# Dissolving the pooling stage into the linear attention stage, and holding the slab pairs by stage

## The reference, cut to what matters

```
p, gla_q, gla_k, gla_v, gla_g, r_f, r_b, q, k, v = split_in(rmsnorm(x) modulated @ w_in)
pooled:  for each of 4 groups of 64 columns, window w in (2, 4, 8, 16):
         m = mean over the window around each token - the token itself
         pooled = (m @ w_pool[group]) * s_pool
linear attention (gla): gates la = log_sigmoid(r @ w_gate + b_gate) / 16, in two directions;
         o = causal decayed attention forwards + strict one backwards; rmsnorm(o, g_gla) * silu(gla_g)
attention: q, k = rmsnorm per head of 64, times g_q, g_k; axial_rope on the latent tokens; softmax attention
```

## Time and profile before

| what | value |
|---|---|
| median of three runs | 4188.84 us |
| the profiled execution's own time | 4184.54 us |
| its span, first to last instruction | 4182.7 us |
| TensorE busy, share of the span | 86% |
| VectorE, ScalarE, GpSimd busy | 54%, 30%, 28% |
| mean granted TensorE clock | 0.917 |
| pooling stage, layer 0 and layer 1, from VectorE's first instruction to that of the next stage | 43.95 us, 44.82 us |
| linear attention, the same | 177.94 us, 144.72 us |

### The profile page before, as it was taken

The page is one execution under the profiler, slowest core; times in us unless marked ns, Lnnn a source line. Parts: engine busy times, 40 slices in busy tenths (PEclk is TensorE's granted clock), DMA queues, the critical chain, the costliest instruction groups (busy, mean ns, idle before and its releaser), DMA issues. The chain is left out here.

```text
span 4182.7 us, 56917 instructions
## 1 busy us (share of the span) xinstructions
PE 3584.2 (86%) x22004; PEld 2999.0 (72%) x22004; DVE 2271.7 (54%) x3290; ACT 1249.8 (30%) x1868; POOL 1160.9 (28%) x564
## 2 busy tenths in 40 slices
PE   6955697899998965798997899888988986887998
PEld 4745576788887745677885788767777775775886
DVE  4658562655655347545445588723666766336334
ACT  4113322221222113323223345432333432323222
POOL 4205002232222203014442333143231230423442
PEclk7977898999999977899998999999999998998998
DMA  4420001223222420013331121121111110212221
GB/s 162 166 79 1 1 1 61 76 96 111 107 85 88 166 79 1 1 41 116 116 115 54 66 70 65 46 91 61 46 42 36 46 37 11 96 65 71 96 95 60
DMA packets 85333, 295.30 MB, mean 71 GB/s; under 512 B 13507, under 2 KB 14083, under 8 KB 84741
## 3 DMA queue, kind: packets, MB, share of 16 engines
q1 hardware_dynamic: 84836, 290.74, 19.7%
q10 hardware_dynamic: 288, 1.60, 0.1%
HBM read 290.21 MB, written 2.10 MB: 70 GB/s over the span
## 5 line engine op out<-in xcount | busy, mean ns | idle before, releaser
L222 POOL TENSOR_TENSOR slab_lo<-slab,slab_hi 128x1024 fp32r<-128x1024 f32 x330 | 823.8, 2502 | 2273.1 <-ACT slab_hi L205 2273.1
L205 ACT ACTIVATE slab_hi<-slab 128x1024 fp32r<-128x1024 f32 x330 | 346.2, 1056 | 792.7 <-PE banks L121 473.7
L119 PE MATMUL banks<-hT_hi,slab_hi 128*128 128x512 f32 (+1 forms) x896 | 354.7, 396 | 44.7 <-POOL slab_lo L222 34.3
L120 PE MATMUL banks<-hT_lo,slab_hi 128*128 128x512 f32 (+1 forms) x896 | 349.5, 390 | 0.0
L121 PE MATMUL banks<-hT_hi,slab_lo 128*128 128x512 f32 (+1 forms) x896 | 349.0, 389 | 0.0
L119 PE MATMUL banks<-mlp_hid_hi,slab_hi 128*128 128x512 f32 (+1 forms) x768 | 282.0, 367 | 10.1 <-DVE mlp_hid_lo L1794 10.1
L1794 DVE TENSOR_TENSOR mlp_hid_lo<-mlp_sq,mlp_hid_hi 128x512 fp32r<-128x512 f32 (+1 forms) x96 | 216.6, 2257 | 120.9 <-ACT mlp_hid_hi L1752 120.5
L120 PE MATMUL banks<-mlp_hid_lo,slab_hi 128*128 128x512 f32 (+1 forms) x768 | 279.6, 364 | 0.0
L121 PE MATMUL banks<-mlp_hid_hi,slab_lo 128*128 128x512 f32 (+1 forms) x768 | 279.4, 364 | 0.0
L119 PE MATMUL banks<-slab_hi,hT_hi 128*128 128x256 f32 (+1 forms) x728 | 246.4, 338 | 2.5 <-ACT rT L872 2.5
L119 PEld LDWEIGHTS banks<-hT_hi,slab_hi 128*128 128x128 f32 x896 | 172.4, 192 | 82.1 <-POOL slab_lo L222 35.7
(11 more groups left out here) (552 smaller groups left out, 8251.7 us busy)
## 6 DMA issues: line engine op xcount, KB each, us to landing
slab<-in_s_mlp_dram SPq DMA_DIRECT2D x192, 512.0 KB, 3.6
proj_vec_slab<-in_s_vec_proj_dram SPq DMA_DIRECT2D x64, 512.0 KB, 3.6
mlp_vec_slab<-in_s_vec_mlp_dram SPq DMA_DIRECT2D x64, 512.0 KB, 3.5
slab<-in_s_ssm_dram SPq DMA_DIRECT2D x48, 512.0 KB, 3.5
slab<-in_s_gdn_dram SPq DMA_DIRECT2D x48, 512.0 KB, 3.5
slab<-in_s_in_dram SPq DMA_DIRECT2D x32, 512.0 KB, 4.6
slab<-in_s_out_dram SPq DMA_DIRECT2D x24, 512.0 KB, 3.7
slab<-in_s_merge_ssm_dram SPq DMA_DIRECT2D x24, 512.0 KB, 3.5
```

Source lines behind the costliest of these rows:

```text
L119: nc.tensor.matmul(out, lhs.hi, rhs.hi, start=start, stop=False)
L120: nc.tensor.matmul(out, lhs.hi, rhs.lo, start=False, stop=False)
L205: self.nc.scalar.activation(hi, self.raw[s][:], ACT.Copy).then_inc(self.rounded, 1)
L222: self.nc.gpsimd.tensor_tensor(pair.lo[:], self.raw[u % slots][:], pair.hi[:].bitcast(F32), ALU.subtract).then_inc(self.split, 1)
```

## The change

The stage `pooling` is removed, and each of its instructions stands in `gla`, spread over its parts:

- SyncE issues the band, gains, rope table and w_pool behind the four loads of the gate weights.
- ScalarE squares q and k in two instructions (tiles 0 to 3 into r3, 4 and 5 into r2) before everything else; the root stands behind the six Abs; the means of the first two groups are moved behind Ln, those of the other two between the exponents of level 1 and level 2. The scaling by s_pool is now ScalarE's, behind the exponents of levels 5 and 8.
- VectorE sums the squares, takes the reciprocal, multiplies by root and gains, and rotates tile 2, all before the gates. It clears F and rotates tile 3 directly behind the gates, before the own products; tiles 4 and 5 are rotated behind the decayed keys, before the masks of the states.
- TensorE makes the first two groups' means behind the gate logits, the others' behind the own products, and mixes behind the products of levels 3 and 6. Banks 6 and 7 are kept for this, so the level products go round six banks.
- The stage's semaphores are 26 before and 37 after; pooling had 12, attention has 11, the end of modulation 1 and the projection 21.
- Ring holds no pairs of its own. Each stage that streams slabs (modulation start, projection, out and post product, mlp, merge, and now also the two scans of the second block) takes as many as it uses, four or three, from its own memory. The added tensors of `gla` lie in the memory that this leaves free.

The diff, cut to its core (the removed function is printed above):

```
-    SLOTS, PAIRS = 4, 3
+    SLOTS = 4
...
-        self.pairs = [sbuf_pair(ctx.enter_context, nc, f"slab{s}", [P, D]) for s in range(self.PAIRS)]
...
-    def fourth_pair(self, stage):
-
-        self.pairs[3:] = [sbuf_pair(stage.held.enter_context, self.nc, f"{stage.name}_slab3", [P, D])]
+    def hold_pairs(self, stage):
+
+        self.pairs = [sbuf_pair(stage.held.enter_context, self.nc, f"{stage.name}_slab{n}", [P, D]) for n in range(self.shape(self.at)[3])]
...
+        m_ = [sb(f"m{n}", [P, TOK]) for n in range(2)]
...
+        qk_sq = [(0, 4, r3[:, 0:4 * nqk * HD]), (4, 6, r2[:, 0:2 * nqk * HD])]
+        pool_loads, wp_loads, qk_loads, wp_cleared, means, moved, mixed, pooled = (sem(n) for n in
+            ("pool_loads", "wp_loads", "qk_loads", "wp_cleared", "means", "moved", "mixed", "pooled"))
+        qk_squared, qk_summed, qk_root = (sem(n) for n in ("qk_squared", "qk_summed", "qk_root"))
...
+                sp.dma_start(rope[:], a["rope"].rearrange("p (s t f) -> p s t f", s=2, t=LAT_TILES)).then_inc(qk_loads, 16)
+                sp.wait_ge(wp_cleared, 2)
+                for g in range(4):
+                    o_ = 64 * (g % 2)
+                    sp.dma_start(wp[o_:o_ + 64, g // 2, o_:o_ + 64], a["w_pool"][l, g]).then_inc(wp_loads, 16)
...
+                def pool_means(pair):
+
+                    if pair:
+                        pe.wait_ge(moved, 3)
+                    else:
+                        pe.wait_ge(pool_loads, 16 + 1)
+                    for n, (t0, t1) in enumerate(((CTX_TILES, C), (0, CTX_TILES))):
+                        for gg_ in range(2):
+                            g = 2 * pair + gg_
+                            for t in range(t0, t1):
+                                same = 0 if t == t0 else 2 if t == t1 - 1 else 1
+                                terms = [(t, same)] + [(t - 1, 3)] * (t > t0) + [(t + 1, 4)] * (t < t1 - 1)
+                                for e, (src, kind) in enumerate(terms):
+                                    last = nc.tensor.matmul(c.ps[64 * gg_:64 * gg_ + 64, 6 + n, (t - t0) * P:(t - t0 + 1) * P],
+                                                            c.tok[:, src, C_POOL + 64 * g:C_POOL + 64 * g + 64],
+                                                            bands[:, kind, g, :], start=e == 0, stop=e == len(terms) - 1)
+                        last.then_inc(means, 1)
+
+                def pool_mix(pair):
+                    pe.wait_ge(wp_loads, 16 * 4 + 1)
+                    pe.wait_ge(moved, 5)
+                    if pair:
+                        pe.wait_ge(pooled, 3)
+                    for n, s in enumerate((slice(CTX, TOK), slice(0, CTX))):
+                        nc.tensor.matmul(c.ps[:, 6 + n, 0:s.stop - s.start], wp[:, pair, :], m_[pair][:, s], start=True, stop=True).then_inc(mixed, 1)
...
+                pool_means(0)
...
+                pool_means(1)
...
                         pe.wait_ge(own_read, nb + 1)
                     for n in range(nb // 2):
                         done = (lev - 1) * (nb // 2) + n
-                        if done >= 8:
-                            pe.wait_ge(a_read, done - 6)
+                        if done >= 6:
+                            pe.wait_ge(a_read, done - 4)
                         for e in range(4):
                             ch = first + 2 * n + e // 2
-                            last = nc.tensor.matmul(c.ps[:, done % 8, e * P:(e + 1) * P].rearrange("p (h f) -> p h f", h=2),
+                            last = nc.tensor.matmul(c.ps[:, done % 6, e * P:(e + 1) * P].rearrange("p (h f) -> p h f", h=2),
                                                     F[:, lev % 2, e % 2, ch * P:(ch + 1) * P], Q[:, lev % 2, :, e % 2, ch, :], start=True, stop=True)
                         last.then_inc(a_full, 1)
+                    if lev in (3, 6):
+                        pool_mix(lev // 3 - 1)
                 pe.wait_ge(a_read, LEVELS * nb + 1)
...
+                def pool_moved(pair):
+                    for n, s in enumerate((slice(CTX, TOK), slice(0, CTX))):
+                        act.wait_ge(means, 2 * pair + n + 2)
+                        nc.scalar.activation(m_[pair][:, s], c.ps[:, 6 + n, 0:s.stop - s.start], ACT.Copy).then_inc(moved, 1)
+
+                def pool_out(pair):
+                    for n, s in enumerate((slice(CTX, TOK), slice(0, CTX))):
+                        act.wait_ge(mixed, 2 * pair + n + 2)
+                        nc.scalar.activation(c.pooled[:, pair, s], c.ps[:, 6 + n, 0:s.stop - s.start], ACT.Copy,
+                                             scale=c.small(l, "s_pool")[:, pair:pair + 1]).then_inc(pooled, 1)
+
+                for t0, t1, sq_ in qk_sq:
+                    nc.scalar.activation(sq_.rearrange("p (t n) -> p t n", t=t1 - t0), x[:, t0:t1], ACT.Square).then_inc(qk_squared, 1)
                 for t in range(C):
                     act.wait_ge(logits, t + 2)
                     nc.scalar.activation(t0_[:, t, :], c.ps[:, t, :], ACT.Abs).then_inc(exps, 1)
+                act.wait_ge(qk_summed, 3)
+                nc.scalar.activation(qk_stat[:, 1, :], qk_stat[:, 0, :], ACT.Sqrt, bias=c.eps, scale=1.0 / HD).then_inc(qk_root, 1)
...
+                pool_moved(0)
...
+                    if lev == 1:
+                        pool_moved(1)
+                    if lev in (5, 8):
+                        pool_out(lev // 3 - 1)
...
+                nc.vector.memset(wp[:], 0.0).then_inc(wp_cleared, 1)
...
+                def rotate(t):
+                    xv = x[:, t].rearrange("p (h r s f) -> p h r s f", h=nqk, r=2, s=2)
+                    x1, x2 = xv[:, :, :, 0, :], xv[:, :, :, 1, :]
+                    cs, sn = (rope[:, j, t - CTX_TILES, :].rearrange("p (r f) -> p r f", r=2).unsqueeze(1).to_broadcast([P, nqk, 2, 16])
+                              for j in range(2))
+                    nc.vector.tensor_tensor(rot[:, 0], x1, sn, ALU.mult)
+                    link(nc.vector.tensor_tensor(rot[:, 1], x2, sn, ALU.mult))
+                    nc.vector.tensor_tensor(x1, x1, cs, ALU.mult)
+                    link(nc.vector.tensor_tensor(x2, x2, cs, ALU.mult))
+                    nc.vector.tensor_tensor(x1, x1, rot[:, 1], ALU.subtract)
+                    link(nc.vector.tensor_tensor(x2, x2, rot[:, 0], ALU.add))
+
+                for n, (t0, t1, sq_) in enumerate(qk_sq):
+                    dve.wait_ge(qk_squared, n + 2)
+                    nc.vector.tensor_reduce(qk_stat[:, 0, t0 * nqk:t1 * nqk], sq_.rearrange("p (n e) -> p n e", e=HD), AX, ALU.add).then_inc(qk_summed, 1)
+                dve.wait_ge(qk_root, 2)
+                link(nc.vector.reciprocal(qk_stat[:, 2, :], qk_stat[:, 1, :]))
+                for t in range(C):
+                    last = nc.vector.tensor_tensor(heads(t), heads(t), qk_stat[:, 2, t * nqk:(t + 1) * nqk].unsqueeze(2).to_broadcast([P, nqk, HD]), ALU.mult)
+                link(last)
+                dve.wait_ge(qk_loads, 49)
+                for t in range(C):
+                    last = nc.vector.tensor_tensor(heads(t), heads(t), g_qk[:], ALU.mult)
+                link(last)
+                rotate(2)
                 dve.wait_ge(exps, C + 3)
                 for t in range(C):
 
                     link(nc.vector.scalar_tensor_tensor(out=la[:, t, :], in0=c.ps[:, t, :], scalar=0.0, in1=t0_[:, t, :],
                                                         op0=ALU.min, op1=ALU.subtract))
                     nc.vector.tensor_scalar(la[:, t, :], la[:, t, :], 1.0 / 16, None, ALU.mult).then_inc(la_ready, 1)
+                dve.wait_ge(la_ready, C + 1)
+                nc.vector.memset(F, 0.0).then_inc(cleared, 1)
+                rotate(3)
 
...
-                nc.vector.memset(F, 0.0).then_inc(cleared, 1)
...
                         last = nc.vector.tensor_tensor(kd[:, 2 * d:2 * d + 2, s], kd[:, 2 * d:2 * d + 2, s], c.gqk[:, 2:4, s], ALU.mult)
                     last.then_inc(kd_ready, 1)
+                rotate(4)
+                rotate(5)
...
-        pooling(c, f"pool{l}", l, a)
         gla(c, f"gla{l}", l, a, first)
         attention(c, f"attn{l}", l, a, update_ctx)
```

117 lines of the change are left out of this document (21 added, 96 removed).

## The result

| kernel | executions | median, us | range, us | ratio to before, 95% interval |
|---|---|---|---|---|
| before | 4 | 4187.33 | 4185.38 to 4190.89 | |
| after | 4 | 4141.2 | 4116.80 to 4152.68 | 0.9877 [0.9851, 0.9902] |
| after, measured again | 6 | 4139.42 | 4124.62 to 4149.03 | 0.987 [0.9839, 0.9901] |
| after, a third time | 8 | 4142.26 | 4123.67 to 4154.47 | 0.9885 [0.9858, 0.9913] |

A forecast was written before the change was run, and what follows sets the result against it. Stages chained by barriers, pooling mostly waiting, VectorE full only in the level loop. Pooling's 88.8 less 5.5, 9.5 and 2.8 gives 71.0 us; 4188.8 - 71.0 = 4117.8, say 4118; own range 4110 to 4128, 8 in 10 4108 to 4132.

The forecast's parts named there:

- 88.8 - 5.5 - 9.5 - 2.8 = 71.0 us: Whole change: 88.8 us of pooling removed, less 5.5 for barriers, 9.5 before the level loop, 2.8 behind it.
- a stretch outside the two layers' attention stages that differs by over 1 us: Sign that the forecast is wrong: any stretch away from both layers' attention stages changing by more than 1 us.
- 15.1 if the means run at clock 0.50: Upper bound of the 9.5 us lost before the level loop: TensorE's means take 2.8 us more in each layer.
- Rival 3: More is won: TensorE gets clock 1.00 in the gates' sums, ScalarE's wait vanishes, tails catch up: 4108 to 4112; 6%.
- Barriers: Semaphore work at linear attention's entry (1.9 us) and exit (0.85), in both layers: 5.5 us back, bounds 4.3 to 6.5.
- Up to the gates: Start of linear attention, T being VectorE's first instruction there: gates start at T+28.7, 4.65 us late.
- rival 1: Linear attention's gains land at T+26 (T: VectorE's first instruction there), gates 5 us later in each layer: 4128; 12%.
- The rotation beside GpSimd: Behind the gates, VectorE's second rotation beside GpSimd's first differences: 4.3 us, 1.5 more than alone; differences 1.8 more.
- the estimate by that rule, 5.2 us: Same rotation, if two-input VectorE instructions and GpSimd exclude each other: about 5.2 us, whole gain 0.5 us smaller.
- The second decayed operands: VectorE's entry to the level loop, behind the second exponent (T+49.7): 4.6 us late in layer 0, 4.9 in layer 1.
- In the loop and behind it: Mixings and moves hidden in the level loop; two rotations behind it cost 1.0 us (layer 0) and 1.8 (layer 1).
- The pairs: Slab pairs at other addresses in the stages that stream slabs: no engine's work altered, zero us.

The follow-up runs named there:

- the later kernel: Kernel after with one extra matmul in each context unit and, in both layers, the norm's gains loaded behind the rope table: 4121.17 us, ratio 0.9833.
- the pair of runs without the fall: One extra matmul in each context unit of layer 0's attention, added to the kernel after (4124.54 us) and to the kernel before (4191.93 us).

## Why the prediction was right and wrong

**What failed is a term that the sum does not have.** "88.8 - 5.5 - 9.5 - 2.8 = 71.0 us" lets softmax attention behind the changed stages cost what it did, without a reason. Even the sign of an error, "a stretch outside the two layers' attention stages that differs by over 1 us", left that stage out. I gave TensorE's clock a price only inside the changed stages ("15.1 if the means run at clock 0.50"), and none in layer 0's attention, which starts 28.8 us earlier after them. There 26.2 us went in the first profile and 19.6 in the second, which is of an execution at the median of its measurement; 19.9 of the 23.4 us between forecast and median are not in the changed stages. It shows in the trace of before that this stage begins at 0.50 and rises 6.5 us in; that the rise can be followed by a fall, the table by stretches did not show. Rival 3 had the clock as a gain only. No rival had it as a loss, though a price was at hand: 16 units, each longer by what TensorE's part of it takes at half the clock.

Supported by runs: a change in attention's own TensorE work alone, more of it or in another order, takes the loss away (4124.5 both times), half the change brings it (layer 0), half doesn't (layer 1), pairs don't (4186.5), and a kernel without the change gets it in most executions from 0.9 us of delay (4211.0). Why the clock falls after a rise at 5.3 to 5.8 us and not at others stays open: the band is an observation on twelve profiles, and I found no edit that sets the moment of the rise at will.

By the steps of the sum:

- **Barriers**, 5.5 forecast. Entries 3.80 and 5.54 against 3.7 and 5.4; exits 4.21 and 4.51 against 3.43 and 3.72 before, 0.78 and 0.79 each where 0.85 stood. 2.00 + 2.00 + 1.57 = 5.6. Right.
- **Up to the gates**, forecast T+28.7; measured T+29.95 and T+29.91. The step that failed is the place of the logits, taken from before, where the first Abs came at T+6.7. After it is T+8.1, and all behind it is later by 1.4:

```profile
271.75 3.78 PE L1010 MATMUL banks<-gla_wg,rT 33*128 33x512 f32 x4 [12.77 <-DMA gla_grow<-in_g_gla_dram]
...
273.86 0.60 ACT L1092 ACTIVATE gla_r<-banks 128x512 f32<-128x512 f32 x1 [4.79 <-PE banks L1010]
...
282.88 0.34 ACT L1094 ACTIVATE gla_qk_stat<-gla_qk_stat,const 128x60 f32<-128x60 f32 x1
```

  I had counted what stands in front of the added transfers and not what the added ones do to those in front. Taking the last of the four small ones out of the wait gave 3.4 us. That the band and the others hold it up is the reading that fits (T+4.6 before, with none behind it); taking them away was not tried. The rest holds: Squares hidden, root behind the sixth Abs, VectorE idle until T+17.5 by it, and **no wait for gains or rope**: rival 1 did not come. How much slack was left is not shown; the 0.70 and 1.60 us of wait in the later kernel are for the transfer moved behind the rope table, with the root some 3 us earlier.
- **The rotation beside GpSimd**, 4.3 forecast, from 305.36 to 310.98, 5.6 us:

```profile
305.70 1.11 DVE L1171 TENSOR_TENSOR gla_rot<-tok,gla_rope 128x320 f32<-128x320 f32 x1
306.85 1.00 DVE L1172 TENSOR_TENSOR tok<-tok,gla_rope 128x320 f32<-128x320 f32 x1
...
305.02 1.45 POOL L1150 TENSOR_TENSOR gla_r<-gla_bT 128x384 f32<-128x384 f32 x1 [86.40 <-ACT gla_bT L1102]
...
306.43 1.07 POOL L1151 TENSOR_TENSOR gla_r<-gla_bT 128x384 f32<-128x384 f32 x1
...
307.46 1.07 POOL L1150 TENSOR_TENSOR gla_r<-gla_bT 128x384 f32<-128x384 f32 x1
```

  0.49 us alone becomes 1.0 to 1.1, and a difference 0.83 becomes 1.07. Both engines go on in step, one instruction each in 1.03 us, where 0.46 and 0.79 are their spacings alone. The measured pair of products (0.96 alone, 1.48 beside GpSimd) was the right row, but I scaled by its ratio, and what it shows is an amount: 0.52 us are added to the product and 0.57 (1.03 less 0.46) to an instruction of the rotation, half as long. Six times 0.52 on top of 2.8 would have been 5.9. The Trainium skill, SBUF — State Buffer, section "Who interferes with whom", has them exclude each other; the estimate by that rule, 5.2 us, was nearer than my 4.3. Full exclusion would be 1.25 us for the pair, so the trace agrees in the main and not to the last fifth.
- **The second decayed operands**: forecast T+49.7, 4.6 late; measured 317.38, T+51.7, 6.5 late. They begin with no wait, so in layer 0 VectorE's own queue set them and not the exponent behind the means, which ended at 315.84. In layer 1 it was as forecast, the exponent (a wait of 0.62 ended by it), 6.1 late where 4.9 stood. The excess is the 1.2 us of the gates and, in layer 0, the rotation too.

```profile
317.38 0.96 DVE L1216 TENSOR_TENSOR gla_r<-gqk,gla_r 128x768 f32<-128x768 f32 x1
...
1563.12 0.69 DVE L1216 TENSOR_TENSOR gla_r<-gqk,gla_r 128x512 f32<-128x512 f32 x1 [0.62 <-ACT gla_r L1106]
```
- **In the loop and behind it**, forecast 1.0 and 1.8. From the second decayed operands to attention, exit barrier aside, layer 0 lost 1.0 and layer 1 2.1. The six banks, mixings and moves are hidden, and the masks run without a wait:

```profile
412.21 3.68 DVE L1256 TENSOR_TENSOR gla_r<-banks,const 128x512 f32<-128x512 f32 x6
...
1633.82 3.68 DVE L1256 TENSOR_TENSOR gla_r<-banks,const 128x512 f32<-128x512 f32 x6
```

- **The pairs**: zero forecast, 0.9993 [0.9977, 1.001] measured.

So of 71.0 us, 67.5 came in the stages, and the pair of runs without the fall agrees; the shortfall is some 1.2 us for the logits in each layer and, in layer 0, the rotation. Some twenty of the 67.5 were lost again next door, in the median.

## What to carry to other kernels

A change that moves a stage in time can change the clock that TensorE is granted in it. Here a stage of short dependent matmuls, which begins at 1.2 GHz behind 10.5 us without TensorE work, ran its context units at either level. Look at the granted clock of the stages behind an edit before the sum is closed, and give that a rival with a price (instructions that are paced by TensorE, times their difference at the two levels). Where the level differs from execution to execution, try a little more TensorE work or another order of the same work: here 3.4 us of work gave back 15, and cost 3 in the kernel that seldom had the loss. When the executions of one kernel stand in two groups, profile one of each.

## What the runs showed of the hardware that I had not expected

- TensorE stayed at 1.2 GHz for 58.1 us of context units and the first latent ones although the profile has it busy in all 58.1; at 2.4 GHz such units kept it busy for 45.9 of 46.0 us and the clock stayed up. So in one and the same code each level was held for 44 us and more.
- 0.91 us of VectorE work in front of a stage cost the kernel before 24 us in the median: 9 of 12 executions were slow, against 3 of 17 beside them without it.
- A small broadcast transfer (32 KB, in pieces of 256 bytes), fourth in its queue, let TensorE start at T+4.6 when nothing was issued behind it and at T+6.1 with 1.25 MB and more behind it; the three in front of it were in by T+2.7.
